# One form of product for the whole input projection of a Mamba-2 mixer, and its chunk carry as a third block of scores

## The reference

```
zxbcdt = u @ w_in                                   # 2048 -> 4096 (z) + 6144 (x, B, C) + 64 (dt)
xbc = silu(causal_dwconv(xbc, conv_w, conv_b))      # 4 taps over time
...
CB = einsum('bclgn,bcsgn->bgcls', Cc, Bc)           # per chunk of 128 tokens, per group
scores = CB[:, :, None] * exp(segsum(A*dt))
y_diag = einsum('bgecls,bcsgep->bclgep', scores, X) # inside a chunk
states = einsum('bclgn,bgecl,bclgep->bcgepn', Bc, decay_states, X)
y_off = einsum('bclgn,bcgepn,bgecl->bclgep', Cc, states_in, exp(A_cs))   # from chunk 0 into chunk 1
y = (y_diag + y_off + d_skip * xs) * silu(z)
y = rmsnorm over groups of 512 (y) * norm_g ;  out = y @ w_out
```

## Time and profile before

| | |
|---|---|
| time, median of 3 runs | 2685.89 us (2684.47 to 2686.33) |
| the profiled execution's own time | 2685.37 us |
| its span in the trace | 2683.7 us |
| PE busy | 2658.5 us, 99% |
| DVE busy | 2001.5 us, 75% |
| ACT busy | 1376.0 us, 51% |
| blocks in three-matmul form (L401) | 1376 |
| blocks in 512-column form (L419) | 5984 |
| granted PE clock, mean | 0.998 |

### The profile page before, as it was taken

The page is one execution under the profiler, slowest core; times in us unless marked ns, Lnnn a source line. Parts: engine busy times, 40 slices in busy tenths (PEclk is TensorE's granted clock), DMA queues, the critical chain, the costliest instruction groups (busy, mean ns, idle before and its releaser), DMA issues.

```text
span 2683.7 us, 47807 instructions
## 1 busy us (share of the span) xinstructions
PE 2658.5 (99%) x16831; PEld 2389.3 (89%) x16831; DVE 2001.5 (75%) x2805; ACT 1376.0 (51%) x1869; POOL 283.2 (11%) x314
## 2 busy tenths in 40 slices
PE   9999999999999999999999999999999999999998
PEld 8999888888888888899998999988888888888887
DVE  7788776665666678889996799978666566667776
ACT  6776444444444445556664566644444444444454
POOL 1001300000000111100001000032000000001211
PEclk9999999999999999999999999999999999999999
DMA  6545565556655566655555655555555665555564
GB/s 215 183 168 193 184 199 188 188 175 189 203 190 190 190 194 196 185 178 193 190 193 181 204 182 192 193 182 189 191 188 174 188 205 190 190 188 176 187 202 138
DMA packets 154237, 504.62 MB, mean 188 GB/s; under 512 B 17104, under 2 KB 21520, under 8 KB 152976
## 3 DMA queue, kind: packets, MB, share of 16 engines
q1 hardware_dynamic: 154048, 503.14, 57.9%
q10 hardware_dynamic: 80, 0.07, 0.0%
HBM read 500.97 MB, written 2.16 MB: 187 GB/s over the span
## 4 chain that ended last, share of the span: by engine, by line
PE 89%; DVE 5%; ACT 3%; issue 2%; DMA 1%; SPq 0%; DVEq 0%; ACTq 0%
PE bank L419 51%; PE bank L421 26%; PE bank L401 4%; PE bank L403 4%; PE bank L402 4%; DVE wlo L923 2%; ACT whi L629 1%; DVE arena L1131 1%; DMA wraw<-in_A 0%; ACT L707 0%; PE bank L592 0%; DVE R L1024 0%; ACT arena L707 0%; ACT arena L716 0%; PE bank L583 0%
## 5 line engine op out<-in xcount | busy, mean ns | idle before, releaser
L419 PE MATMUL bank<-R,whi 128*128 128x512 f32 x5984 | 2083.4, 394 | 0.1
L421 PE MATMUL bank<-R,wlo 128*128 128x256 f32 x5984 | 1662.6, 278 | 0.0
L923 DVE TENSOR_TENSOR wlo<-wraw,whi 128x1024 fp32r<-128x1024 f32 (+2 forms) x1008 | 1164.0, 1161 | 547.4 <-ACT whi L629 545.9
L629 ACT ACTIVATE whi<-wraw 128x1024 fp32r<-128x1024 f32 (+2 forms) x1008 | 984.3, 983 | 912.8 <-PE bank L421 810.4
L419 PEld LDWEIGHTS bank<-R,whi 128*128 128x128 f32 x5984 | 1122.0, 188 | 259.9 <-DVE wlo L923 0.4
L421 PEld LDWEIGHTS bank<-R,wlo 128*128 128x128 f32 x5984 | 1124.8, 188 | 0.1
L401 PE MATMUL bank<-R,whi 128*128 128x256 f32 x1376 | 393.2, 286 | 5.5 <-DVE wlo L923 5.2
L403 PE MATMUL bank<-R,wlo 128*128 128x256 f32 x1376 | 389.5, 283 | 0.0
L402 PE MATMUL bank<-R,whi 128*128 128x256 f32 x1376 | 389.4, 283 | 0.0
L401 PEld LDWEIGHTS bank<-R,whi 128*128 128x128 f32 x1376 | 262.5, 191 | 10.2 <-DVE wlo L923 5.6
L402 PEld LDWEIGHTS bank<-R,whi 128*128 128x128 f32 x1376 | 262.7, 191 | 0.2
(11 more groups left out here) (177 smaller groups left out, 1271.7 us busy)
## 6 DMA issues: line engine op xcount, KB each, us to landing
wraw<-in_F SPq DMA_DIRECT2D x352, 512.0 KB, 3.3
wraw<-in_B SPq DMA_DIRECT2D x224, 512.0 KB, 3.3
wraw<-in_A SPq DMA_DIRECT2D x96, 512.0 KB, 3.8
wraw<-in_F SPq DMA_DIRECT2D x128, 384.0 KB, 3.1
wraw<-in_F SPq DMA_DIRECT2D x128, 320.0 KB, 3.2
wraw<-in_PL SPq DMA_DIRECT2D x64, 512.0 KB, 4.0
arena<-cs_rows SPq DMA_DIRECT2D x8, 1024.0 KB, 5.7
arena<-in_gates SPq DMA_DIRECT2D x8, 512.0 KB, 3.7
```

What stands on the lines that cost most here:

```text
L419: nc.tensor.matmul(dst.rearrange("p (s t) -> p s t", s=2), whi[:, q % RING, cols], src[:, :, k, :], start=first, stop=False)
L421: mm = nc.tensor.matmul(dst[:, 0:SEQ], wlo[:, q % RING, cols], src[:, 0, k, :], start=False, stop=last)
L629: nc.scalar.activation(whi[:, slot, 0:w * BLOCK], wraw[:, slot, 0:w * BLOCK], ACT.Copy).then_inc(w_hi, 1)
L923: V.tensor_tensor(wlo[:, slot, 0:w * BLOCK], wraw[:, slot, 0:w * BLOCK], whi[:, slot, 0:w * BLOCK].bitcast(F32), ALU.subtract).then_inc(w_ ...
```

## The change

- The 512-column form is used in all of B1. Each finished tile now has two halves: ACT copies the low half out of the bank at every odd q, once piece q is used (`low_half`, new L842), DVE adds the other half to it (new L1316), does the last tap of the tile before, and scales (new L1322). The taps and silus are spread: taps 2 and 1 at the even step with the previous tile's silu between them, tap 0 at the next odd step. The last silu is at DVE's step 14, behind `lo`.
- PE's C*B products and transposes come after piece 15, DVE's reading of them is at step 16, the score products at steps 17 and 18.
- The block from chunk 0 to chunk 1 becomes a third block of scores: `csb` has 384 columns a head, ACT makes 6 Relus of 128x128 and one exponential of 128x768 for two heads, the score products are 128x1536, and PE adds a third product for each head into the same bank. `xdec`, `cross`, `ebc` with its transfers and exponential, and the four carry products go.
- In every norm ACT takes the square root straight from PSUM and DVE the reciprocal after it. At the very end DVE scales 12 of the 16 tiles of the output and GpSimd 4.

```diff
-WIDE = ("A2", "F1", "F2", "B2")
-LAST = ((0, 4), (4, 4), (8, 4), (12, 2), (14, 2))
+WIDE = ("A2", "B1", "F1", "F2", "B2")
+LAST = ((0, 3), (3, 3), (6, 3), (9, 2), (11, 1))
+LAST_POOL = ((12, 2), (14, 2))
...
-        csb = scratch(2048).rearrange("p (e t) -> p e t", e=GROUP_HEADS)
+        csb = scratch(GROUP_HEADS * 3 * CHUNK).rearrange("p (e t) -> p e t", e=GROUP_HEADS)
...
+        low_half = scratch(2 * SEQ).rearrange("p (n t) -> p n t", n=2)
...
-                            sp.dma_start(csb, cs_dram[at(group * GROUP_HEADS, GROUP_HEADS), :]
+                            sp.dma_start(csb[:, :, 0:SEQ], cs_dram[at(group * GROUP_HEADS, GROUP_HEADS), :]
...
-                            if not (first and ph["half"] == 0):
-                                sp.wait_ge(y_done_state, group)
-                            for e in range(2):
-                                sp.dma_start(ebc[64 * e:64 * e + 64],
-                                             cs_dram[at(group * GROUP_HEADS, GROUP_HEADS), CHUNK:SEQ]
-                                             .rearrange("(j e) t -> e j t", e=2)[e:e + 1].broadcast_to([64, 4, CHUNK])
-                                             ).then_inc(eb_in, 16)
...
-                    if ph["name"] not in WIDE and not (ph["name"] == "B1" and q >= 12 or gate):
+                    if ph["name"] not in WIDE and not gate:
...
-                            if q == 14:
+                            if q == 15:
                                 pe.wait_ge(silu_done, group * 6 + 6)
...
                             if q == 19:
-                                pe.wait_ge(xdec_done, group + 1)
                                 pe.wait_ge(sc_done, group * 2 + 2)
-                                for j in range(4):
-                                    mm = nc.tensor.matmul(bank[5][:, j * CHUNK:(j + 1) * CHUNK], xdec[:, j * P:(j + 1) * P],
-                                                          cross, start=True, stop=True)
-                                mm.then_inc(carry_mm, 1)
                                 for j in range(4):
...
-                                        mm = nc.tensor.matmul(dst[rows, cols + CHUNK:cols + SEQ], xtok[:, 1, ch],
-                                                         csb[:, head, CHUNK:SEQ], start=True, stop=True)
+                                        nc.tensor.matmul(dst[rows, cols + CHUNK:cols + SEQ], xtok[:, 1, ch],
+                                                         csb[:, head, CHUNK:SEQ], start=True, stop=False)
+                                        mm = nc.tensor.matmul(dst[rows, cols + CHUNK:cols + SEQ], xtok[:, 0, ch],
+                                                         csb[:, head, SEQ:SEQ + CHUNK], start=False, stop=True)
...
-                act.wait_ge(var_done, k + 1)
-                nc.scalar.activation(rinv[:], rinvh[:], ACT.Sqrt).then_inc(rinv_done, 1)
+                act.wait_ge(stats_done, k + 1)
+                nc.scalar.activation(rinvh[:], bank[6][:, 0:SEQ], ACT.Sqrt, bias=eps[:, 0:1], scale=1.0 / D
+                                     ).then_inc(root_done, 1)
...
+                            if q % 2 == 1:
+                                act.wait_ge(w_used, p + 1)
+                                act.wait_ge(bank_free, it * 10 + ph["group0"] + 4 + q // 2 - 1)
+                                nc.scalar.activation(low_half[:, q // 2 % 2, :], bank[BANKS4[q // 2 % 4]][:, SEQ:2 * SEQ],
+                                                     ACT.Copy).then_inc(half_done, 1)
...
-                            if q == (11 if very_first else 9):
-                                act.wait_ge(eb_in, group * 32 + 32)
-                                nc.scalar.activation(ebc, ebc, ACT.Exp).then_inc(ebc_done, 1)
...
                                 e0 = q - 11
 
                                 for e in (e0, e0 + 1):
-                                    for c in range(2):
+                                    for c in (2, 0, 1):
                                         r = nc.scalar.activation(csb[:, e, c * CHUNK:(c + 1) * CHUNK],
-                                                                 csb[:, e, c * CHUNK:(c + 1) * CHUNK], ACT.Relu,
+                                                                 csb[:, e, min(c, 1) * CHUNK:(min(c, 1) + 1) * CHUNK], ACT.Relu,
                                                                  bias=cst[:, c, at(group * GROUP_HEADS + e)], scale=-1.0)
                                 own.link(r)
...
+            nc.scalar.activation(spare[:], ones[:, 0:1], ACT.Sqrt)
...
-                dve.wait_ge(stats_done, k + 1)
-                own.link(V.tensor_scalar(rinvh[:], bank[6][:, 0:SEQ], 1.0 / D, EPS, ALU.mult, ALU.add))
-                V.reciprocal(rinvh[:], rinvh[:]).then_inc(var_done, 1)
-                dve.wait_ge(rinv_done, k + 1)
-                if k == 6:
-                    return
+                dve.wait_ge(root_done, k + 1)
+                own.link(V.reciprocal(rinv[:], rinvh[:]))
...
+                        if name == "B1" and q == 14:
+                            conv_silu(it + ph["half"] * 4, 5)
...
-                                later_taps(cpad[:, nt % 2], ca[:, nt, :],
-                                           lambda k, nt=nt, group=group: flat(bpar[:, at(group), nt * 5 + k:nt * 5 + k + 1]),
-                                           conv_done)
-                            if q % 2 == 0 and 4 <= q <= 12 or q == 13:
-                                nt = (q + 1) // 2 - 2
-                                dve.wait_ge(conv_t, group * 6 + nt + 1)
-                                V.scalar_tensor_tensor(out=ca[:, nt, :], in0=cth[:, nt % 2, :], scalar=1.0,
-                                                       in1=ca[:, nt, :], op0=ALU.add, op1=ALU.mult).then_inc(silu_done, 1)
+                                second = tap(group, nt, 2)
+                                if nt:
+                                    conv_silu(group, nt - 1)
+                                own.need(second)
+                                third = tap(group, nt, 1)
                             if q % 2 == 1:
-                                dve.wait_ge(w_used, p + 1)
-                                src = bank[BANKS4[q // 2 % 4]][:, 0:SEQ]
-                            if q % 2 == 1 and q < 12:
-                                nt = q // 2
-                                V.tensor_tensor(cpad[:, nt % 2, 3:3 + SEQ], src, rinv[:], ALU.mult).then_inc(bank_free, 1)
-                            if q % 2 == 1 and q > 12:
-                                j = q // 2 - 6
-                                if j == 0 and not very_first:
+                                tile = q // 2
+                                dst = cpad[:, tile % 2, 3:3 + SEQ] if tile < 6 else zt[:, tile - 6, :]
+                                dve.wait_ge(half_done, group * 10 + tile + 1)
+                                if tile == 6 and not very_first:
                                     dve.wait_ge(yn_lo, group * 4)
-                                fold(BANKS4[q // 2 % 4], zt[:, j, :])
-                                V.tensor_tensor(zt[:, j, :], zt[:, j, :], rinvh[:], ALU.mult).then_inc(bank_free, 1)
+                                folded = own.mark(V.tensor_tensor(dst, bank[BANKS4[tile % 4]][:, 0:SEQ], low_half[:, tile % 2, :],
+                                                                  ALU.add))
+                                if 1 <= tile <= 6:
+                                    own.need(third)
+                                    last_tap(group, tile - 1)
+                                own.need(folded)
+                                V.tensor_tensor(dst, dst, rinv[:] if tile < 6 else rinvh[:], ALU.mult).then_inc(bank_free, 1)
                             if q in (14, 16, 18):
-                            if q == 14:
+                            if q == 16:
                                 dve.wait_ge(turned, group + 1)
...
-                                V.tensor_tensor(by_head(xdec), by_head(xtok[:, 0, :]), per_head(wdt[:, heads]),
-                                                ALU.mult).then_inc(xdec_done, 1)
...
-                            if q in (15, 17):
-                                h0 = 0 if q == 15 else 4
+                            if q in (17, 18):
+                                h0 = 0 if q == 17 else 4
                                 dve.wait_ge(exp_done, group * 4 + h0 // 2 + 2)
-                                if q == 15:
+                                if q == 17:
                                     own.need(own.latest())
                                 V.tensor_tensor(csb[:, h0:h0 + 4, :], csb[:, h0:h0 + 4, :],
                                                 cbm.rearrange("p c l -> p (c l)").rearrange("p (e n) -> p e n", e=1)
-                                                .broadcast_to([P, 4, SEQ]), ALU.mult).then_inc(sc_done, 1)
...
+                def tap(group, nt, k):
```

(23 more changed lines are left out.)

105 lines of the change are left out of this document (51 added, 54 removed).

## The result

| | before | after |
|---|---|---|
| time, median | 2686.11 us (2684.38 to 2688.14, 6 runs) | 2756.64 us (2754.73 to 2757.29, 6 runs) |
| ratio | | 1.0258 (95%: 1.0247 to 1.0269) |
| span of the profiled execution | 2683.7 us | 2755.6 us |
| mean granted PE clock | 0.998 | 0.989 |
| DVE, ACT busy | 2001.5, 1376.0 us | 1998.9, 1418.9 us |

The changed kernel is 2.6% slower, 70 us where 40 were forecast, and outside the range of 2702 to 2746 us. From the page after: busy times, and groups that the change made or enlarged (busy, mean ns, idle before).

A forecast was written before the change was run, and what follows sets the result against it. It took PE, busy for all of a group's 61.90 us, to bound the input phase. The profiled 2685.37 us + 42.7 (input phase) - 1.7 (ending and norms) gave 2726.4, predicted as 2726 us; 8-in-10 range 2702 to 2746.

The forecast's parts named there:

- The silu's wait: PE waits before the C*B products for the last silu: 3.2 us without lag, 4.9 us in a steady group.
- The scores' wait: PE waits before the y products for the second score product: 2.1 us a group, bounds 1.8 and 2.4.
- The clock falls in the waits (13%): Rival, 13%: PE drops to half speed after silu waits, 2 to 3 us each, +12 to +20: 2738 to 2746.
- The lag: ACT and DVE run late at piece 11 after the last group's norm: 1.7 us added to the silu's wait.
- PE's saving: PE's own work in the input phase gets shorter: -1.3 us a group, between -0.2 and -1.6.
- +0.87 - 0.99: Terms of PE's work a group: 8 more y products +0.87 us, the four carry products gone -0.99 us.
- The other norms: New norms give ACT's `hi` back some 2 us sooner, counting only at the start: -0.5 us (0 to -0.9).
- The ending: At the end DVE scales 12 of 16 tiles, 3.53 us for 4.70: -1.2 us (bounds 0 and -1.7).
- By group: Input phase: six groups +5.7 us each, first of the second half +4.0, very first +4.5; sum +42.7.
- The inner bounds of 2716 to 2737: Range of the sum as worked out (55%), from lag 0.7 to 2.5 us and PE between -0.2 and -1.6.
- Its chain of links: Serial ACT and DVE steps added up: 14.3 us from piece 11's end, 7.6 us from piece 17's end.

The follow-up runs named there:

- e2: The changed kernel with 16 unused 128x128 products of ones on PE behind piece 15, ahead of the wait for the silu: 2741.1 us.
- e6: The changed kernel with the last silu ahead of `lo` at step 14 and ACT's decay factors ahead of the low-half copies: 2726.3 us.
- e9: e7 with the old group norm, scale and reciprocal at DVE's step 5, ahead of the root: 2682.3 us.
- e7: The changed kernel with silu ahead of `lo`, decay factors at steps 7, 9, 11, 15, broadcast two pieces sooner, reading at 15, score products at 15 and 17: 2691.0 us.
- e3: The changed kernel without the 512-column form in B1; third block of scores, new norms and new ending stay: 2685.7 us.
- e11: The kernel before with the wide form alone, its work spread, and the change's ending (root from PSUM in the last norm alone) in five stores: 2676.9 us.
- e1: The changed kernel with the convolution's last silu ahead of `lo` of DVE's step 14, no longer behind it: 2745.6 us.
- e5: The changed kernel with ACT's decay factors at steps 11, 13, 15, 17 ahead of the low-half copy of the same step: 2744.2 us.
- e10: e7 without its spread factors: decay factors left at steps 11, 13, 15, 17, broadcast not asked for sooner: 2704.6 us.

## Why the prediction was wrong

It had the direction, both waits, their places and their releasers. By its own steps:

- **The silu's wait**, forecast 4.9 us in a steady group: 4.6 to 5.5. The links were as priced: from start to next start six Relus 1.88 and the exponential 0.75 (forecast 1.89 and 0.75), and the score product lasts 1.75.
- **The scores' wait**, forecast 2.1: 1.66 to 1.78.
- **"The clock falls in the waits (13%)" was the failed step.** I took the rival as the unlikely case, and argued from the 2.57 us wait of the earlier trace rows, that had gone unpunished, to waits twice as long, of which the trace had none. It is the largest term missed: 15.5 us by e2. Nor are short waits safe: in e6 two waits of 2.42 us brought 3.4 us at half rate each. The rival itself was priced right, 2 to 3 us for each wait and 12 to 20 in all. The Trainium skill (TensorE: Matmul & The Clock Gate, "Why this matters for your kernels") has the rule that idle gaps between bursts bring the half rate back; the trace after agrees, with 0.50 from 1353.40 to 1356.40. I cited it and set it aside.
- **The lag.** I saw that the reciprocal moves to step 7, and gave it 1.7 us of lag before the silu's wait, but not a wait of its own. The new norm made one before piece 11, 0.6 to 1.1 us in the six steady groups, 4.5 us in all (e9).
- **PE's saving**, forecast -1.3 us a group. The 24 products of y take 3.04 us to the next block, where the carry and 16 products took 2.93: I had +0.87 - 0.99, it is +0.11. And each wait costs about 0.16 us more than the idle time that the view gives: from 1332.62 to 1333.83 are 1.21 us, where a block and the wait make 0.35 + 0.70, since the idle time is counted from the recorded end of the last product, 0.28 us behind its start, and the next one follows after 0.12 when nothing is waited for. The first block behind the wait then takes 0.46 us for 0.35. In e9, with nearly no waits, a group is 61.5 for 61.9.
- **The other norms**, forecast -0.5 us: in the profiled executions PE reaches the norm ahead of the input phase at 1157.83 us after the change and 1157.15 before, +0.7. Kernels with the new norms reach it at 1156.9 (e7) to 1158.6 (e3), so there is no gain that can be measured.
- **The ending**, forecast -1.2 us: +0.3. DVE's scaling did fall from 4.70 to

```profile
2747.34 3.61 DVE L1404 TENSOR_TENSOR h<-arena,bank 128x768 f32<-128x768 f32 x5
```

  but DVE's scaling is not what ends the kernel (e11).
- **By group**: +5.7 forecast in the six steady groups, +9.6 and +10.0 measured (half 1, half 2); +4.0 in the first of the second half, +5.4; very first +4.5, +5.6. The input phase cost 70 us for 42.7. Of the 27 us that were missed, the clock is 15.5, the wait before piece 11 is 4.5, and PE's smaller saving, with what each wait costs beyond its idle time, most of the rest. With the clock's 15.5 us the forecast would have been about 2742, still in its range; it took the smaller terms, all missed in the same direction, to leave it. The inner bounds of 2716 to 2737 don't follow from the two terms that they name: a lag of 0.7 to 2.5 us is -6 to +5 over six groups and PE's saving -2.4 to +8.8 over eight, so about 2718 to 2740; nothing here turns on it.

What the prediction didn't ask is which edit causes the loss. Its chain of links read as if each link were worth its own length. e1, e5 and e6 show that a link taken out of one loop is worth a fraction (10 us for 36 of silu's wait), because the next loop is as full, and e10 and e7 that the same links cost next to nothing in other steps: 2691.0 us with all of them still there, 0.14% above the kernel before.

## What to carry to other kernels

Where two engines hand work to and fro for a third, add up each one's list between the last point with slack and the point of need, not only the wait that shows: removing a wait moves it to the next need, until work is moved ahead of the full stretch, or to where it no longer stands in a row at its end. Two edits that are each free or cheap can cost far more together, since they spend the same slack: nothing and +26 us here, +70 together. And a wait of several microseconds on PE costs more than its length: price the half rate behind it as part of the likeliest case.
